# Expert products of a two-layer model by Strassen's scheme: seven block products in place of eight

## The reference, cut to what matters

```python
def expert_block(args):
    xs, es, gs = args
    h = jax.nn.gelu(jnp.einsum('td,thkd->thk', xs, u[es]), approximate=False)
    return jnp.einsum('thk,thkd->td', gs * h, v[es])
```

## Time and profile before

| What | us |
|---|---|
| Median of 3 runs (5256.15 to 5261.77) | 5261.64 |
| Span of the profiled execution | 5254.7 |
| PE busy in it | 4763.7 (91%) |
| DVE busy | 3114.3 (59%) |
| ACT busy | 1674.3 (32%) |
| POOL busy | 359.2 (7%) |
| Stage `experts` of the first layer | from 1172 to 2608 |

### The profile page before, as it was taken

The page is one execution under the profiler, slowest core; times in us unless marked ns, Lnnn a source line. Parts: engine busy times, 40 slices in busy tenths (PEclk is TensorE's granted clock), DMA queues, the critical chain, the costliest instruction groups (busy, mean ns, idle before and its releaser), DMA issues. The chain is left out here.

```text
span 5254.7 us, 99504 instructions
## 1 busy us (share of the span) xinstructions
PE 4763.7 (91%) x39436; PEld 4576.9 (87%) x39436; DVE 3114.3 (59%) x6332; ACT 1674.3 (32%) x2572; POOL 359.2 (7%) x196
## 2 busy tenths in 40 slices
PE   7777796999999999999887768969999999999998
PEld 7656695989999999999885557959899999999998
DVE  3555488865555555547735554888655555555577
ACT  2332223863222222222123322238622222222222
POOL 0200153000000000000002001530000000000000
PEclk9978898999999999999988788989999999999999
DMA  2330121674333333325323311216733333333353
GB/s 94 106 154 9 75 96 39 206 212 163 117 117 117 117 125 130 120 106 181 127 79 125 123 41 47 92 64 193 224 138 117 126 130 119 117 117 117 112 193 122
DMA packets 390914, 631.78 MB, mean 120 GB/s; under 512 B 29208, under 2 KB 327728, under 8 KB 348848
## 3 DMA queue, kind: packets, MB, share of 16 engines
q1 hardware_dynamic: 388688, 620.75, 33.5%
q10 hardware_dynamic: 2016, 8.26, 0.4%
HBM read 526.53 MB, written 152.36 MB: 129 GB/s over the span
## 5 line engine op out<-in xcount | busy, mean ns | idle before, releaser
L228 PE MATMUL ex_op<-ex_ah,ex_vl 128*128 128x288 f32 x3584 | 1062.6, 296 | 7.6 <-DVE ex_acc L2364 6.4
L230 PE MATMUL ex_op<-ex_ah,ex_vh 128*128 128x288 f32 x3584 | 1058.2, 295 | 0.0
L229 PE MATMUL ex_op<-ex_al,ex_vh 128*128 128x288 f32 x3584 | 1057.2, 295 | 0.0
L2364 DVE TENSOR_TENSOR ex_acc<-ex_acc,ex_op 128x576 f32<-128x576 f32 x896 | 673.0, 754 | 547.5 <-PE ex_op L230 540.5
L228 PE MATMUL ex_hp<-x_hi,ex_ul 128*128 128x288 f32 x3072 | 906.8, 295 | 17.2 <-PEq L122 17.2
L230 PE MATMUL ex_hp<-x_hi,ex_uh 128*128 128x288 f32 x3072 | 907.3, 295 | 0.0
L229 PE MATMUL ex_hp<-x_lo,ex_uh 128*128 128x288 f32 x3072 | 906.5, 295 | 0.0
L228 PEld LDWEIGHTS ex_op<-ex_ah,ex_vl 128*128 128x128 f32 x3584 | 673.4, 188 | 15.1 <-DVE ex_acc L2364 15.1
L230 PEld LDWEIGHTS ex_op<-ex_ah,ex_vh 128*128 128x128 f32 x3584 | 673.5, 188 | 0.0
L229 PEld LDWEIGHTS ex_op<-ex_al,ex_vh 128*128 128x128 f32 x3584 | 673.2, 188 | 0.0
L2313 ACT ACTIVATE ex_vh<-ex_v 128x2048 fp32r<-128x2048 f32 x128 | 245.6, 1919 | 1139.7 <-PE ex_op L230 859.9
(11 more groups left out here) (418 smaller groups left out, 8787.3 us busy)
## 6 DMA issues: line engine op xcount, KB each, us to landing
ex_u<-in_peer_uT SPq DMA_DIRECT2D x128, 1024.0 KB, 7.6
ex_v<-in_peer_v SPq DMA_DIRECT2D x128, 1024.0 KB, 6.8
gate_matrix<-g_stage SPq DMA_DIRECT2D x18, 4096.0 KB, 15.9
ex_g<-gate_matrix SPq DMA_DIRECT2D x128, 576.0 KB, 5.0
dec_k<-in_cache_kT SPq DMA_DIRECT2D x16, 1536.0 KB, 10.8
dec_v<-in_cache_v SPq DMA_DIRECT2D x16, 1536.0 KB, 8.0
out_s_k<-in_cache_k_kept SPq DMA_DIRECT2D x128, 190.5 KB, 6.2
out_s_v<-in_cache_v_kept SPq DMA_DIRECT2D x128, 190.5 KB, 6.3
```

The lines of the kernel that those rows point to most:

```text
L228: nc.tensor.matmul(out, w_lo, x_hi, start=first, stop=False)
L229: nc.tensor.matmul(out, w_hi, x_lo, start=False, stop=False)
L230: return nc.tensor.matmul(out, w_hi, x_hi, start=False, stop=last)
L2364: nc.vector.tensor_tensor(a, a, o[:, :, 0:HALF], ALU.add).then_inc(s.added, 1)
```

## The change

Both products of `experts` are made by Strassen's scheme (the variant with shared sums). The product of a 2x2 arrangement of blocks takes seven block products ("units") in place of eight, on sums of the weights' corners and sums of the other operand.

- A block of work is 7 units of 12 matmuls (84). A first block makes U x of one group, with the corners of U (two halves of D, two expert blocks) and of x (two halves of D, two token halves). A second block makes half of the outputs for two groups. Per layer there are 48 first and 64 second blocks, 112 in all, in 16 turns: `turn` has two second blocks, a first one, two second ones and two first ones. The last turn has only four second blocks, and three first blocks stand ahead of the first turn.
- The split weights lie in a ring of seven slots of 128x512 elements, one for each unit; a slot is refilled for the next block when its unit is done. PE waits before each unit for its slot.
- Per block POOL makes 4 sums of corners in the raw buffer (128x512 each, both inputs in SBUF) and 3 low parts (128x512, both inputs in SBUF): 7 instructions. ACT makes the high parts (one of 1024 elements, five of 512). DVE makes 3 low parts (one of 1024 elements, two of 512).
- DVE adds a unit's result into the sum (`result`, 128x576 from PSUM) after each unit of a second block, with two buffers in PSUM. PE's unit u waits for the result of unit u - 2. After a first block it makes 3 combinations from PSUM (`combine`), and ACT 4 copies (`take`).
- The gated hidden values need 4 more operands that are sums (`hidden_sum`, 128x576) and 7 splits per pair of groups (`hidden_high`, `hidden_low`, 128x576 each). Gates are multiplied over 128x1152 at once. Sums of x are made once, ahead of the first block (`token_high`, `token_low`, `whole_tokens`).
- The raw weights lie in the place of `h`, which is stored to `kept_h` in `gates` and loaded again at the end. `low(NU)` and `high(NU)` of `gates` are gone. The early hidden values are spread over the turns.

The core of the diff:

```diff
+    READY = (3, 3, 3, 4, 5, 6, 7)
+    LOWS = {0: 1, 1: 1, 4: 2, 6: 3, 2: 1, 3: 2, 5: 3}
+    ON_POOL = (2, 3, 5)
+        raw = m.h[:].rearrange("p i d -> p (i d)").rearrange("p (b c) -> p b c", b=2)
...
+                def second_block(b, v, pair, half):
+                    for u in range(UNITS):
+                        n = v.at * UNITS + u
+                        weights_ready(b, u)
+                        if half == 0:
+                            pe.wait_ge(s.al, pair.times(UNITS, READY[u]))
+                        reach(pe, s.read_v, v.times(UNITS, u - 1))
+                        w_hi, w_lo = ring(u)
+                        for j in range(2):
                             for e in range(EG):
+                                c = slice(e * 2 * P + j * P, e * 2 * P + (j + 1) * P)
+                                ins = three_passes(nc, op[:, n % 2, j, 0:HALF], w_hi[:, c], w_lo[:, c],
+                                                   a_hi[:, u, e, :], a_lo[:, u, e, :], e == 0, e == EG - 1,
+                                                   u in (3, 4, 5))
+                        ins.then_inc(s.unit, 1)
...
+                def high(b, u):
+                    if u in SUMS:
+                        act.wait_ge(s.summed, b.times(4, SUMS[u]))
+                    else:
+                        act.wait_ge(raw_in[b.parity()], b.halved(32, 32))
+                    reach(act, s.unit, b.times(UNITS, (1 if u == 0 else u) - 6))
...
+            @block.gpsimd
+            def _(pool):
+                def add(b, out, x, y):
+                    out, x, y = (corner(b, place) for place in (out, x, y))
+                    nc.gpsimd.tensor_tensor(out, x, y, ALU.add).then_inc(s.summed, 1)
+                def low(b, u):
+                    pool.wait_ge(s.hi, b.times(UNITS, u + 1))
+                    hi, lo = (by_rows(w, b) for w in ring(u))
+                    nc.gpsimd.tensor_tensor(lo, corner(b, PLACE[u]), hi.bitcast(F32),
+                                            ALU.subtract).then_inc(s.lo_pool, 1)
+                def prepare(b, between=None):
+                    pool.wait_ge(raw_in[b.parity()], b.halved(32, 32))
+                    add(b, SUM, A21, A22)
+                    add(b, A21, A11, A21)
+                    pool.wait_ge(s.lo_dve, b.times(3, 1))
+                    pool.wait_ge(s.summed, b.times(4, 2))
+                    add(b, A11, SUM, A11)
+                    low(b, 2)
+                    pool.wait_ge(s.summed, b.times(4, 3))
+                    add(b, A12, A11, A12)
+                    low(b, 3)
+                    low(b, 5)
...
+                    b, v = t.block(1), t.values(1)
+                    gate(t.gate(0), 1, 0, gelud=t.first(-1))
+                    result(b, v, 1, 0, first)
+                    low(b, 6)
+                    result(b, v, 1, 1, first)
+                    hidden_low(nxt, 1)
+                    result(b, v, 1, 2, first)
+                    low(b.plus(1), 0)
+                    result(b, v, 1, 3, first)
+                    hidden_sum(nxt, 2)
+                    result(b, v, 1, 4, first)
+                    hidden_low(nxt, 2)
+                    result(b, v, 1, 5, first)
+                    low(b.plus(1), 4)
+                    result(b, v, 1, 6, first)
```

More of the change, by code:

```diff
@@ L2222, in load_early @@
[L2222 to L2237, removed]
+                def turn(t, last=False):
+                    second_weights(t.block(2) if last else t.block(3), odd_groups(t), 0)
+                    if not last:
+                        gate_values(t.gate(1), t.first(0).times(1, EARLY))
+                    keep(t.of(4).times(1))
+                    second_weights(t.block(3) if last else t.block(4), odd_groups(t), 1)
+                    keep(t.of(4, 1).times(1))
+                    if last:
+                        keep(t.of(4, 2).times(1))
+                        keep(t.of(4, 3).times(1))
+                        return
+                    first_weights(t.block(5), t.first(1))
+                    gate_values(t.gate(2), t.of(1, 1).times(1))
+                    first_weights(t.block(6), t.first(2))
+                    early(t)
+                    keep(t.of(4, 2).times(1))
+                    second_weights(t.block(7), even_groups(t.next()), 0)
+                    gate_values(t.gate(3), t.first(1).times(1, EARLY))
+                    second_weights(t.block(8), even_groups(t.next()), 1)
+                    gate_values(t.gate(4), t.first(2).times(1, EARLY))
+                    keep(t.of(4, 3).times(1))
@@ new lines, in _ @@
+                second_weights(Count(4), (EARLY, EARLY + 1), 1)
+                gate_values(before.gate(4), EARLY + 2)
+                first_weights(Turn(0).block(2), Turn(0).first(0))
+                turn(Turn(0))
+                with sp.Fori(0, (LAST - 1) // 2) as i:
+                    for o in (1, 2):
+                        first_weights(Turn(o, i).block(2), Turn(o, i).first(0))
+                        turn(Turn(o, i))
+                turn(Turn(LAST), True)
+                sp.wait_ge(s.lo_dve, 3 * BLOCKS)
@@ L2301, in _ @@
+                for q in range(3):
+                    first_block(Count(q), Count(q), q == 0)
+                turn(Turn(0))
+                with pe.Fori(0, (LAST - 1) // 2) as i:
+                    for o in (1, 2):
+                        turn(Turn(o, i))
+                turn(Turn(LAST), True)
             @block.scalar
             def _(act):
[L2303 to L2307 removed]
@@ L2417, in _, with low @@
-                add(NG - 1, range(KD), True)
+                def low(b, u):
+                    dve.wait_ge(s.hi, b.times(UNITS, 2 if u == 0 else u + 1))
+                    if u == 0:
+                        hi, out = (by_rows(w, b, 2) for w in slots(0, 2))
+                        src = top_corners(b)
+                    else:
+                        hi, out = (by_rows(w, b) for w in ring(u))
+                        src = corner(b, PLACE[u])
+                    nc.vector.tensor_tensor(out, src, hi.bitcast(F32), ALU.subtract).then_inc(s.lo_dve, 1)
@@ new lines, in _ @@
+                low(b.plus(1), 4)
+                combine(b, Count(1), 2, 0, 1)
+                hidden_low(Count(0), 2)
+                last_of_pair(Count(2), Count(2), Count(0), before.gate(3), Count(1))
+                turn(Turn(0), first=True)
+                with dve.Fori(0, (LAST - 1) // 2) as i:
+                    for o in (1, 2):
+                        turn(Turn(o, i))
+                turn(Turn(LAST), last=True)
+                dve.wait_ge(s.read_v, 4 * (LAST + 1) * UNITS)
+                for t in (lo_half, hi_half):
+                    nc.vector.tensor_tensor(acc[:, 4:8, t], acc[:, 4:8, t], both[:], ALU.subtract)
```

744 lines of the change are left out of this document (557 added, 187 removed).

## The result

The changed kernel takes 5866.0 us (median; 5864.5 to 5876.6), the kernel before 5258.9 us: a ratio of 1.1157 (95% interval 1.1142 to 1.1173), 607 us more. The forecast was 5600 us, with a range up to 5850. The direction was right; the size was 266 us short, and the time lies 16 us above the range.

The account below looks back on a forecast made before the run. PE was taken to bound `experts` before; after, mutually excluding DVE and POOL work (92.1 us) plus 6.6 unused makes 98.7 us a turn. 16 turns plus 25.5 of edges, +168.6 a layer, give 5600 us; range 5120 to 5850.

Parts of the forecast that it names:

- What bounded the kernel, and what PE gains: Stage `experts`: PE alone sets the end; its work per turn falls from 89.1 to 78.0 us.
- Rival 2: Stage `experts`: PE stays the bound, POOL's work fitting beside DVE's PSUM reads and idle time; 78.0 us a turn, 4936; chance 0.12.
- The raw weights have two buffers ...: nothing: Weight loads in `experts`: a period of 14 us for a landing of 7.6 us, so no cost.
- The loads of the engines: Per turn in `experts`: ACT 46 us, DVE 66, POOL 63.2, each fitting alone in PE's 78.
- They don't run alone: In `experts`, DVE and POOL instructions with both inputs in SBUF exclude each other; the waiting one is 0.13 us shorter afterwards.
- The sum: 92.1 + 6.6 = 98.7: Turn of `experts`: 92.1 us of mutually excluding DVE and POOL work plus 6.6 us unused makes 98.7 us.
- 1.1 us unused in a block: Played DVE and POOL lists of a second block: some 1.1 us unused, in six of seven blocks, 6.6 us a turn.
- Edges: Start and end of `experts`: 10.5 us of before, +12 and +3, 25.5 us a layer; median 6.9 us above the span.
- The clock: PE's granted clock in `experts`: costs nothing while its mean stays over 0.79; below that it would bind.
- Rival 1: POOL in `experts` takes 1.06 us on 512 elements; 87.4 us a turn, 5237, or 5132 with unused time halved; chance 0.15.
- Rival 3: DVE and POOL in `experts` exclude each other in full, plus other waits: 109.9 us a turn, 5957; chance 0.10.
- Rival 4: The change doesn't reach the path, since something else than PE bound `experts`; chance under 2 in 100.

Follow-up runs that it names:

- e2: On top of e1, all 49 POOL instructions of a turn work on 64 of 512 elements, the rest left out: 5017.5 us.
- e1: Changed kernel with the load of the early hidden values issued ahead of the loads of blocks 5 and 6: 5679.5 us, ratio 1.0804 to the kernel before.
- e4: On top of e1, each POOL instruction of a turn works on 64 elements and seven constant writes, reading nothing, fill the rest: 5017.6 us.
- e6: On top of e1, POOL's 21 low parts of a turn are made by DVE, nothing left out: 5809.0 us, ratio 1.1027 to the kernel before.
- e3: On top of e1, only POOL's 21 low parts of a turn work on 64 of 512 elements, sums stay whole: 5292.8 us.
- e5: On top of e1, DVE's low part of slot 4 for the next block comes after result 6 in second blocks: 5691.2 us.
- e8: On top of e1, Strassen's scheme kept for the second product alone, the first made plainly: 5590.4 us, ratio 1.0632 to the kernel before.
- e9: Like e8, but POOL's 31 instructions of a turn are made by DVE: 5631.4 us, ratio 1.0704 to the kernel before.
- e7: On top of e1, DVE makes POOL's 28 sums and 21 low parts of a turn, POOL idle: 5715.9 us, ratio 1.0864 to the kernel before.

## Why the prediction was wrong in size, step by step

- **What bounded the kernel, and what PE gains.** Right: 9408 matmuls. With the exclusion gone PE sets the end, but at 81.0 us a turn (e2), not 78.0: PE is busy for 796.48 of the 808.74 us of ten turns, at a granted clock of 1.00, so its own pace in these blocks is 79.6 us and not 78.0. Rival 2's time, 4936, would have been e2's 5018.
- **"The raw weights have two buffers ...: nothing" and the moved loads at nothing.** This step failed, and it is most of the error. The landing time was weighed against the period of the weights, but not the order in which SP issues: the early load was behind two loads that wait for buffers. That cost 7.0 us of DVE's time a turn (the unused time is 13.7 us and not 6.6), and e1 gave 187 of the 266 us back.
- **The loads of the engines.** POOL 49 x 1.26 = 61.7 us (63.2 forecast), results at 745 ns (754). DVE's work was sized well: in e4 40.1 us with both inputs in SBUF (40.1 forecast) and 26.0 us that read PSUM (26.1). Together they are 62.4 us and not 66, since the start of an instruction is recorded under the end of the one before: 3.7 us in some 84 instructions.
- **They don't run alone.** Right, and shown by e2 and e4 against e1. The Trainium skill's rule ("SBUF — State Buffer", section "Who interferes with whom") says that a DVE instruction with two SBUF inputs contends with a GpSimd instruction that reads SBUF, not with one that only writes it, and that one with at most one SBUF input, outside the two-port modes, doesn't contend. The traces agree in both: POOL's writes leave DVE's busy time in a turn at 62.4 us (e4; 62.0 in e2), and the results from PSUM keep 745 ns.
- **The sum: 92.1 + 6.6 = 98.7.** With the load moved the turn is 100.6 to 100.75 us, 2 us more, and both terms nearly hold one by one: 93.2 us of path and 7.5 unused in e1. The first term owes something to luck: 49 x 1.26 + 40.1 = 101.8 us undisturbed where 103.3 was taken, and 8.6 us of it lie side by side where 11.2 were counted as given back. What doesn't carry over is the second term: it was put at some 6 us for e6 too and measured 22.8, and 14.0 in e3. It was small, it seems, only while POOL had work most of the time (77.1 of 100.6 us in e1, 43.8 of 105.5 in e6).
- **1.1 us unused in a block.** The size was right (7.5 us a turn for 6.6), and for 4.3 us of it the place too, POOL's wait for `low(., 0)`. That it is DVE's wait at `low(b.plus(1), 4)` was the reading of the expectation for e5, and is wrong. In e1 PE takes 14.5 us for a second block on average, as the played lists gave (14.5), and 17.1 for the single first block between them, the one with 10 two-input instructions of DVE; in the changed kernel the load's wait brings the second blocks to 16.2.
- **Edges.** 25.5 us a layer; the stage fits them with a turn of 107.0. The median was put 6.9 us above the span; the execution that gave the span stands 1.8 us above it in the changed kernel (5864.5 and 5862.7), an error of 5 us.
- **The clock.** 0.92 in the stage, over the 0.79 from which PE alone would bind. That it costs nothing, as forecast, isn't shown: the mean hides stretches at 0.50, 16.4 us of a turn in the changed kernel and 9.6 in e1, and DVE waits for PE in them for 2.3 and 1.8 us. This could be a part of the 2 us that e1's turn is over the forecast, and of the difference between e6 (18.1 us at 0.50, DVE waiting 4.1 us in them) and e1. No run separates it.
- **The rivals.** Rival 1 fell: POOL takes 1.26 us and not 1.06, so 128 partitions go with the line through the longer shapes. Rival 2 fell by the exclusion. Rival 3, exclusion in full, gave a turn of 109.9 us and 5957, and the 107.0 measured lies nearer to it than to the forecast; but that nearness was the load's, since e1 changes nothing in the exclusion and has 100.75; the path of 103.3 us in this rival is 10 us over the 93.2 measured. Rival 4 never stood.

In one sentence: the mechanism was right, and what failed is that the moved loads were put at nothing, where one of them cost 7.0 us a turn. The range up to 5850 covered twice the unused time but no DMA wait at all; one such wait in each turn, of a landing time, would have given 98.7 + 7 = 105.7 and 5824.

## What to carry to other kernels

When a change reorders loads, write down the order of issue on the queue and for each load the wait of the one ahead of it; a load of a free buffer behind one that waits was late here by 7.0 us in each turn, from its issue to its landing. Work with two inputs in SBUF that goes from DVE to POOL is not taken off DVE while DVE does work of that kind (49 instructions here were worth 36 us of 5716), so a saving of matmuls that is paid in such work has to be set against two sums: what excludes each other (right to 1 or 2 us in e1 and e6), and all that DVE does itself, its PSUM reads and its own waits included. The larger one makes the turn. A mean clock over the bound isn't enough either: look at the granted clock just behind PE's waits. Where engines run hand-written lists with two result buffers, compare block by block and not by the turn's mean: e8 and e9 fit on average and lost 16 to 18 us a turn.

## What the runs showed of the hardware that wasn't expected

- A POOL that only writes (64 elements a time, 149 ns each) is free of charge for DVE: POOL is busy for 50.4 us of a turn in e4 against 21.1 in e2, DVE for 62.4 against 62.0, with 5017.6 against 5017.5 us in all.
- A DVE low part of 512 elements goes from 720 ns (e4) to 1249 ns (e1) on average beside a POOL that reads, but each reading instruction of POOL costs DVE 0.41 us and not its 1.26: the rest lies beside what DVE does undisturbed (its PSUM reads) or doesn't do (its waits). How it is divided among these wasn't measured.
- Fewer reading instructions on POOL don't cost less in proportion: in e6 there are 28 instead of 49, and DVE's 93.3 us are 62.4, 21 more instructions at 0.58 us (12.1; e7 has 49 more than e4 for 28.2 us), and 18.8 us of being shut out: 0.67 us each.
- PE's granted clock fell to 0.50 behind a wait of 4.22 us (e8, from 1767.3 to about 1773 us) and was at 1.00 from 1773 us on, after it had worked without a break; a matmul started each 0.24 us at the lower level and each 0.13 us at the higher.
